# Split weights stored column by column in turn and loaded with a step of two, moving operand and PSUM output walked from the last column to the first

## The reference

```python
def swiglu(h, wg, wu, wd):
    return (jax.nn.silu(h @ wg) * (h @ wu)) @ wd

def trunk(x, p, pos, ...):
    for i in range(DEPTH):                       # DEPTH = 2
        hn = rmsnorm(x, w['norm_mix_g'][i])
        if i < N_A_LAYERS: o = s5_mixer(hn, ...)     # ends with g @ w_glu (2048 x 4096)
        else:              o = nsa_mixer(hn, ...)    # hn @ w_q, ..., o @ w_o (2048 x 2048)
        x = x + o
        x = x + swiglu(rmsnorm(x, w['norm_ffn_g'][i]), w['ffn_w_gate'][i],
                       w['ffn_w_up'][i], w['ffn_w_down'][i])      # D_FF = 5632
        gate = jax.nn.sigmoid(rmsnorm(x, w['norm_ple_g'][i]) @ w['ple_w_gate'][i])
        x = x + gate * (p[i] @ w['ple_w_proj'][i])
        if i == N_A_LAYERS - 1:
            kv = build_kv(x)                     # rmsnorm(x) @ kv_w
```

## Time and profile before

| | |
|---|---|
| median of 3 runs | 3314.52 us (3307.37 to 3318.4) |
| profiled execution, its own time | 3305.81 us |
| its span, first to last instruction | 3304.0 us |
| TensorE matmul (PE) busy | 3222.4 us, 98% |
| TensorE weight load (PEld) busy | 3072.9 us, 93% |
| VectorE (DVE) busy | 2034.2 us, 62% |
| ScalarE (ACT) busy | 1461.7 us, 44% |
| GpSimd (POOL) busy | 539.7 us, 16% |
| mean granted TensorE clock | 0.992 of 2.4 GHz |

### The profile page before, as it was taken

The page is one execution under the profiler, slowest core; times in us unless marked ns, Lnnn a source line. Parts: engine busy times, 40 slices in busy tenths (PEclk is TensorE's granted clock), DMA queues, the critical chain, the costliest instruction groups (busy, mean ns, idle before and its releaser), DMA issues.

```text
span 3304.0 us, 69206 instructions
## 1 busy us (share of the span) xinstructions
PE 3222.4 (98%) x27708; PEld 3072.9 (93%) x27708; DVE 2034.2 (62%) x2281; ACT 1461.7 (44%) x1927; POOL 539.7 (16%) x477
## 2 busy tenths in 40 slices
PE   7999999999999999999999999998999999999998
PEld 6898889899999999999999997855999999999998
DVE  7999988865655544555665546455655554455566
ACT  4555555643543433343454433344444343334444
POOL 5666566620000000000000006000000000000000
PEclk9999999999999999999999999999999999999999
DMA  6445544455556555655556559888555655665553
GB/s 179 142 146 156 165 151 151 133 168 174 181 178 182 172 189 179 180 172 189 172 178 194 182 185 301 287 283 293 179 182 175 184 179 183 179 178 181 181 171 131
DMA packets 384392, 608.42 MB, mean 184 GB/s; under 512 B 52537, under 2 KB 144986, under 8 KB 383882
## 3 DMA queue, kind: packets, MB, share of 16 engines
q1 hardware_dynamic: 360954, 555.84, 53.9%
q10 hardware_dynamic: 20176, 44.08, 4.0%
q0 software_dynamic: 3024, 5.22, 0.4%
HBM read 594.83 MB, written 26.94 MB: 188 GB/s over the span
## 4 chain that ended last, share of the span: by engine, by line
PE 79%; DVE 13%; POOL 2%; issue 2%; ACT 2%; DMA 1%; SPq 0%; DVEq 0%; POOLq 0%; ACTq 0%
PE psum L399 22%; PE psum L401 22%; PE psum L400 22%; DVE rows_rest L1337 2%; DVE turned L1396 2%; PE psum L2312 2%; POOL prod_pool L1550 2%; PE psum L1016 1%; PE psum L2322 1%; DVE normed_chunk L1421 1%; DVE turned L1387 1%; PE psum L2360 1%; DVE state_ri L1404 1%; PE psum L1037 1%; PE psum L1038 1%
## 5 line engine op out<-in xcount | busy, mean ns | idle before, releaser
L384 DVE TENSOR_TENSOR w_rest<-w_raw,w_head 128x1024 fp32r<-128x1024 f32 x776 | 974.1, 1267 | 958.7 <-ACT w_head L380 957.9
L380 ACT ACTIVATE w_head<-w_raw 128x1024 fp32r<-128x1024 f32 x776 | 812.4, 1057 | 1047.3 <-PE psum L401 1015.9
L399 PE MATMUL psum<-act_head,w_head 128*128 128x264 f32 x4224 | 1206.0, 286 | 5.0 <-DVE act_rest L2743 5.0
L401 PE MATMUL psum<-act_head,w_rest 128*128 128x264 f32 x4224 | 1202.0, 285 | 0.0
L400 PE MATMUL psum<-act_rest,w_head 128*128 128x264 f32 x4224 | 1200.2, 284 | 0.0
L399 PEld LDWEIGHTS psum<-act_head,w_head 128*128 128x128 f32 x4224 | 796.8, 189 | 5.9 <-issue 5.4
L400 PEld LDWEIGHTS psum<-act_rest,w_head 128*128 128x128 f32 x4224 | 798.9, 189 | 0.2
L401 PEld LDWEIGHTS psum<-act_head,w_rest 128*128 128x128 f32 x4224 | 797.4, 189 | 0.0
L399 PE MATMUL psum<-hid_head,w_head 128*128 128x264 f32 x1408 | 401.0, 285 | 0.0
L401 PE MATMUL psum<-hid_head,w_rest 128*128 128x264 f32 x1408 | 400.6, 285 | 0.0
L400 PE MATMUL psum<-hid_rest,w_head 128*128 128x264 f32 x1408 | 399.9, 284 | 0.0
(11 more groups left out here) (421 smaller groups left out, 4075.2 us busy)
## 6 DMA issues: line engine op xcount, KB each, us to landing
w_raw<-in_ffn_w_gate SPq DMA_DIRECT2D x176, 512.0 KB, 3.8
w_raw<-in_ffn_w_up SPq DMA_DIRECT2D x176, 512.0 KB, 4.2
w_raw<-in_ffn_w_down SPq DMA_DIRECT2D x176, 512.0 KB, 3.7
w_raw<-in_cache_cmp_k SPq DMA_DIRECT2D x256, 128.0 KB, 2.6
w_raw<-in_cache_cmp_v SPq DMA_DIRECT2D x256, 128.0 KB, 2.6
w_raw<-in_ssm_w_glu SPq DMA_DIRECT2D x64, 512.0 KB, 4.1
w_raw<-in_ple_w_gate SPq DMA_DIRECT2D x64, 512.0 KB, 4.3
tiles<-in_cache_slc_v SPq DMA_DIRECT2D x128, 256.0 KB
```

The lines of the kernel that those rows point to most:

```text
L380: nc.scalar.activation(WH[:, u.slot, :], RAW[:, u.slot, :], ACT.Copy).then_inc(head_done, 1)
L384: nc.vector.tensor_tensor(WL[:, u.slot, :], RAW[:, u.slot, :], WH[:, u.slot, :].bitcast(F32), ALU.subtract).then_inc(rest_done, 1)
L399: nc.tensor.matmul(o, WH[:, u.slot, w], heads[:, k, :], start=k == 0, stop=False)
L401: last = nc.tensor.matmul(o, WL[:, u.slot, w], heads[:, k, :], start=False, stop=k == UK * kunits - 1)
```

## The change

The 1024 columns of a unit are no longer stored tile after tile in `w_head` and `w_rest`. Two neighbouring tiles (2q and 2q+1) share a block of 256 words, and their columns are stored in turn: column c of the even tile at word 2c, of the odd one at word 2c+1. ScalarE and VectorE read `w_raw` as before, and write (VectorE also reads `w_head`) with a step of two words. A matmul of `group_matmuls` loads its tile with a step of two words. Its moving operand is read from column 263 down to column 0, and its PSUM output is written from column 263 down to column 0 as well, so that each result lands where it did before.

The number of instructions on each engine and their order are the same as before, and so are the DMAs, the semaphores and the buffers. Nothing else reads `w_head` and `w_rest` of these units.

```diff
+    def tiles_of(t, u):
+        return t[:, u.slot, :].rearrange("p (q e c) -> p q e c", e=2, c=P)
+
+    def pairs(t, u):
+        return t[:, u.slot, :].rearrange("p (q c e) -> p q e c", e=2, c=P)
+
     def split_head(act, u):
         act.wait_ge(raw_ready[u.slot], 16 * u.turn)
         if not (u.known and u.n < TAP_UNITS + RING):
             act.wait_ge(units_used, u.n - (RING - 1) - TAP_UNITS)
-        nc.scalar.activation(WH[:, u.slot, :], RAW[:, u.slot, :], ACT.Copy).then_inc(head_done, 1)
+        nc.scalar.activation(pairs(WH, u), tiles_of(RAW, u), ACT.Copy).then_inc(head_done, 1)
 
     def split_rest(dve, u):
         dve.wait_ge(head_done, u.n + 1)
-        nc.vector.tensor_tensor(WL[:, u.slot, :], RAW[:, u.slot, :], WH[:, u.slot, :].bitcast(F32),
+        nc.vector.tensor_tensor(pairs(WL, u), tiles_of(RAW, u), pairs(WH, u).bitcast(F32),
                                 ALU.subtract).then_inc(rest_done, 1)
@@ group_matmuls
+                head, rest = heads[:, k, ::-1], rests[:, k, ::-1]
                 for n in range(4):
-                    w = slice(kk * UN + n * P, kk * UN + (n + 1) * P)
-                    o = PSUM[:, bank + n, 0:T]
-                    nc.tensor.matmul(o, WH[:, u.slot, w], heads[:, k, :], start=k == 0, stop=False)
-                    nc.tensor.matmul(o, WH[:, u.slot, w], rests[:, k, :], start=False, stop=False)
-                    last = nc.tensor.matmul(o, WL[:, u.slot, w], heads[:, k, :], start=False,
-                                            stop=k == UK * kunits - 1)
+                    tile = 2 * kk + n // 2
+                    wh, wl = pairs(WH, u)[:, tile, n % 2, :], pairs(WL, u)[:, tile, n % 2, :]
+                    o = PSUM[:, bank + n, T - 1::-1]
+                    nc.tensor.matmul(o, wh, head, start=k == 0, stop=False)
+                    nc.tensor.matmul(o, wh, rest, start=False, stop=False)
+                    last = nc.tensor.matmul(o, wl, head, start=False, stop=k == UK * kunits - 1)
```

## The result

The changed kernel takes 3294.43 us (median of 4 runs, 3292.46 to 3295.86) against 3312.76 us before (4 runs, 3307.37 to 3318.4): ratio 0.9944, interval 0.9929 to 0.9959.

What follows compares the result with a forecast made beforehand. The prediction took the pace of the dense matmuls as the bound; every term was 0, so 3305.81 us stayed about 3306, or 3314 us as a forecast for a median, with a range of 3304 to 3390.

Steps and rivals of the forecast that it cites:

- What bounds the kernel: Dense matmuls: their pace of 121.6 ns is the time, 2265 us of 3304.0; each nanosecond is worth 18.6 us.
- Moving operand read backwards: Stream of each dense matmul: reading it backwards adds 0; bound above 100 ns for 264 columns.
- the read needs no tidy start: Two stage 1 runs of 23, starting at an even word or one later, both 0.120 us a start; supports 0.
- A faster pace: Rival, dense matmuls: if two reads conflict and the new walk parts them, 8 ns each, 149 us less, 3165; chance 0.04.
- Weights loaded with a step of two: Weight load of each dense matmul: the step adds 0, since a load already takes 0.81 ns a column.
- My upper bound of 46 ns: Weight load of each dense matmul: at most 0.36 ns more for each of 128 columns, 0.86 ms in all.
- PSUM written backwards: Output of each dense matmul: writing it backwards adds 0; bound above 100 ns.
- The splits: ScalarE and VectorE accesses with a step of two: add 0; bound above 0.80 us a split, 20 us in the chain.
- The share of `w_rest` in the chain from 660 to 1980 us: Sign to check in the changed kernel's trace: this share, 1.0% before, stays unchanged.
- The first 10 ns are hidden: Dense matmuls: 264 columns stream in 110 ns, so a slower stream's first 10 ns cost nothing, each further one 18.6 us.

Runs made afterwards that it cites:

- stepped_store_only: Kernel before, but splits write with a step of two while matmuls still load 128 adjacent words, everything forwards: ratio 1.0002 to before.
- backward_only: Changed kernel with the splits and weight slices of before; moving operand read and PSUM written backwards: ratio 0.995 to before.
- shorter_stream: `backward_only` with 232 columns instead of 264 moved in every matmul except those of a group's first 128 features: ratio 0.9497.
- alternate: Changed kernel with only odd units stored and loaded with a step of two, even ones as before, stream backwards: 3288.02 us, ratio 0.9922.
- weights_step2_only: Changed kernel with moving operand and PSUM output walked forwards as before, weights still stored and loaded with a step of two: ratio 1.0054.

## Why the prediction was wrong

- **What bounds the kernel: right.** The pace of the dense matmuls decided the time, and 18.6 us for each nanosecond held: 1.24 ns gave 23 us, of which 9 were lost again in the longer distances.
- **"Moving operand read backwards. ... I take 0": the step that failed.** The value was -0.88 ns a matmul (121.73 to 120.85), 16 us. I had weighed only what the backward walk might add. I read the pace of 121.6 ns as what a matmul costs, though 120.1 ns is enough where the addresses are good, and 1.6 are a collision of two reads. The evidence offered for "the read needs no tidy start", the two runs of stage 1 of equal length, compared sums: inside these two runs the single distances go from 115 to 125 and from 118 to 124 ns.
- **"A faster pace (0.04)": the right kind of mechanism with the wrong size and too small a chance.** I priced it at 8 ns from the transposes, and gave it next to no chance since "No row shows such a conflict". The trace shows it when it is sorted: the distances under 160 ns spread from 117 to 127 ns before (5% to 95%), and by the class of the chunk their means run from 120.4 to 123.7. It was worth 1.24 ns of the 1.6 there are, 23 us and not 149.
- **Weights loaded with a step of two, 0: near in this kernel, and by luck.** Forwards it costs 0.93 ns, 17 us; with the backward stream it gains 0.36 ns, 7 us. No term of the sum let one pattern's price depend on another's. The Trainium skill (SBUF — State Buffer, on cachelines) asks for two hits on a 16-byte line. The runs agree with that limit: a load takes 188 ns with adjacent words, 195 with a step of two (two hits), 330 with a step of four (one hit). My upper bound of 46 ns, from a narrower load in another mode with a step of nine, was no bound: a step of four cost 112 ns.
- **PSUM written backwards, 0: right**, 1.0 (0.999 to 1.001). The warning of the Trainium skill (SBUF — State Buffer, on cachelines) on non-contiguous PSUM patterns is not borne out for a backward run.
- **The splits, 0: right for VectorE**, 1.27 us either way, step two on one read and the write. The Trainium skill (Vector Engine (DVE) Microarchitecture Reference, Measured stream behaviour on trn2) asks for adjacent pairs at full rate; by these rows a step of two words does without. ScalarE's head was mis-sized: 0.12 us more instead of 0; it is hidden, since `stepped_store_only` came out at 1.0002. The share of `w_rest` in the chain from 660 to 1980 us, which was to stay at 1.0%, went to 1.4%; but it is 1.7% in `backward_only`, whose splits are those of before, so the stepped splits are not the reason.
- **"The first 10 ns are hidden": not borne out.** In `shorter_stream` the pace fell by 8.6 ns, so at 264 columns the stream's length was in the pace already. (A slip beside it, of no weight: (1.92 - 0.29) / 14 is 0.116 us and not 0.117.)

What stays open: why the pairs collide as they do. The order of the four layouts fits a load that walks its words downwards: then the two reads pass each other by 520 words (step two, forwards), 392 (before), 136 (backwards) and 8 (both) in a matmul, and the pace stands 2.7, 1.7, 0.85 and 0.5 ns over 120. But the same four fit as well the other way round: if the load walks upwards, the words by which the two reads pass each other are 8, 136, 392 and 520 in the same order, and the collision would cost more the longer the two go side by side. The two runs meant to test that at other distances were bound by the load itself, and a load in the other direction was not tried. That the addresses' difference decides, with a period of 256 bytes at the resolution of these chunks, is shown; the direction of the load is open, and so is what inside the memory collides.

## What to carry to other kernels

When matmuls follow each other without a wait, look at the spread of the distances between their starts and not only at the mean. A spread of some nanoseconds at one shape is a hint that something else than the shape is in the pace; here sorting by operand address, modulo 256 bytes, found it. A backward moving operand and a weight layout chosen by address (`alternate`) took away 1.44 of the 1.6 ns, 0.8% of the time, without a single instruction less. A change of layout can cost when alone and pay beside another (the step of two: +0.93 and -0.36 ns), so try all four combinations before one is dropped.

## What was not expected of the hardware

- The weight load of the next matmul and the stream of the present one disturb each other by up to 5 ns of 120 on the mean of a class (class 6 of `weights_step2_only`, 125.1 ns). It repeats: the mean distances at a unit's 24 places are the same within 0.1 ns in the kernel before and in `stepped_store_only`, although ScalarE's splits take longer there.
- A load of 128 fp32r columns: 188 ns with adjacent words, 195 with a step of two, 330 with a step of four; a matmul starts each 120 to 123 ns with the first two, and each 234 ns with the last.
- A ScalarE copy of 1024 elements takes 1.06 us with adjacent writes, 1.15 to 1.18 us with a step of two words; VectorE's subtraction takes 1.27 us with either.
- PSUM written from the last column to the first costs nothing: ratio 1.0 (0.999 to 1.001), pace 121.72 against 121.73 ns.
